# Output projection by tiles with the transposes among its products, and a last norm whose transposes and scaling are spread over three engines

## The reference

```
x = x + mix @ w_out
h = rmsnorm(x, norm_ffn_g)
q = h @ peer_w_q                     # 16 query parts of 128 columns
s = q . sub_keys, top 16 of 128 each # then pairs, gates by softmax
x = x + sum over 16384 experts: gate * gelu(u . h) * v
y = rmsnorm(x, norm_final_g)
```

## Time and profile before

| | before |
|---|---|
| three runs, us | 2292.63, 2301.97, 2316.4 |
| median, us | 2301.97 |
| span of the profiled execution, us | 2299.7 |
| mean granted TensorE clock | 0.955 |
| TensorE busy, us | 2145.2 |
| VectorE busy, us | 1526.3 |
| ScalarE busy, us | 713.2 |

### The profile page before, as it was taken

The page is one execution under the profiler, slowest core; times in us unless marked ns, Lnnn a source line. Parts: engine busy times, 40 slices in busy tenths (PEclk is TensorE's granted clock), DMA queues, the critical chain, the costliest instruction groups (busy, mean ns, idle before and its releaser), DMA issues.

```text
span 2299.7 us, 34370 instructions
## 1 busy us (share of the span) xinstructions
PE 2145.2 (93%) x13939; PEld 1759.0 (76%) x13939; DVE 1526.3 (66%) x2722; ACT 713.2 (31%) x859; POOL 393.5 (17%) x348
## 2 busy tenths in 40 slices
PE   5999998777789998999999999999999999999995
PEld 2545555656654676988989889989899999999995
DVE  2113355676642589888899899898676666666664
ACT  2112232334211201333444444445322222222221
POOL 4000000000000000022233223122332333333330
PEclk8999987778899999999999999999999999999998
DMA  5120110000212211457778779778998888888862
GB/s 183 37 74 19 48 57 14 2 7 2 80 48 106 75 41 38 149 200 268 290 285 316 279 273 335 277 259 293 370 353 309 310 310 310 310 308 311 314 251 97
DMA packets 164278, 437.38 MB, mean 190 GB/s; under 512 B 11968, under 2 KB 77248, under 8 KB 153792
## 3 DMA queue, kind: packets, MB, share of 16 engines
q1 hardware_dynamic: 116064, 242.81, 30.2%
q0 software_dynamic: 36864, 134.23, 15.7%
q10 hardware_dynamic: 11232, 58.73, 6.2%
HBM read 368.57 MB, written 67.17 MB: 189 GB/s over the span
## 4 chain that ended last, share of the span: by engine, by line
PE 56%; DVE 12%; ACT 2%; issue 1%; DMA 0%; POOL 0%; ACTq 0%; DVEq 0%
PE bank L1600 27%; PE bank L1538 21%; PE bank L1547 3%; PE bank L1465 3%; DVE sc L2097 1%; DVE si L2096 1%; DVE si L2099 1%; DVE u_lo L2104 1%; DVE isel L2239 1%; DVE sv L2095 1%; DVE sv L2098 1%; DVE sca L2110 1%; DMA sca<-in_pu_rows,pick 0%; ACT u_hi L921 0%; PE bank L1519 0%
## 5 line engine op out<-in xcount | busy, mean ns | idle before, releaser
L1538 PE MATMUL bank<-xhi,u_hi 128*128 128x448 f32 x1024 | 385.7, 377 | 8.3 <-DVE u_lo L2104 7.7
L1600 PE MATMUL bank<-w_hi,v_hi 128*128 128x448 f32 x1024 | 375.0, 366 | 5.5 <-DVE w_lo L2342 5.5
L1538 PE MATMUL bank<-xhi,u_lo 128*128 128x448 f32 x1024 | 375.5, 367 | 0.0
L1538 PE MATMUL bank<-xlo,u_hi 128*128 128x448 f32 x1024 | 375.0, 366 | 0.0
L1600 PE MATMUL bank<-w_lo,v_hi 128*128 128x448 f32 x1024 | 374.7, 366 | 0.0
L1600 PE MATMUL bank<-w_hi,v_lo 128*128 128x448 f32 x1024 | 374.6, 366 | 0.0
L619 POOL DMA_INDIRECT sca<-in_pu_rows,pick x128 | 173.2, 1353 | 728.8 <-DVE sdot L2110 441.5
L619 POOL DMA_INDIRECT rows_v<-in_pv,pick x128 | 196.1, 1532 | 430.5 <-DVE xs L2324 384.3
L2348 DVE TENSOR_TENSOR v_lo<-v_raw,v_hi 128x4096 fp32r<-128x4096 f32 x32 | 141.6, 4425 | 173.3 <-ACT v_hi L982 173.3
L982 ACT ACTIVATE v_hi<-v_raw 128x4096 fp32r<-128x4096 f32 x32 | 116.1, 3627 | 428.6 <-PE bank L1600 409.6
L1051 PE MATMUL bank<-xnT,wbuf 128*128 128x512 f32 x416 | 230.8, 637 | 0.0
(11 more groups left out here) (524 smaller groups left out, 3103.4 us busy)
## 6 DMA issues: line engine op xcount, KB each, us to landing
u_raw<-in_pu SPq DMA_DIRECT2D x64, 1024.0 KB, 5.0
v_raw<-in_pv SPq DMA_DIRECT2D x32, 2048.0 KB, 17.0
act_scratch<-actb ACTq DMA_DIRECT2D x64, 448.0 KB, 6.0
gate_scratch<-gst ACTq DMA_DIRECT2D x14, 2048.0 KB, 8.7
wts<-act_scratch SPq DMA_DIRECT2D x32, 896.0 KB, 4.8
gring<-gate_scratch SPq DMA_DIRECT2D x32, 896.0 KB, 8.5
wbuf<-in_w_in SPq DMA_DIRECT2D x4, 2048.0 KB, 10.2
wring<-in_w_q SPq DMA_DIRECT2D x4, 2048.0 KB, 8.5
```

The source lines that it names most:

```text
L1538: ins = mm(bank[b][:, 0:DS], lhsT, rhs[:, 0:DS], **on)
L1600: ins = mm(bank[c][:, 0:DS], lhsT, rhs[q][:, e, :], **on)
```

## The change

In the passage the output projection runs tile by tile: `jj` 0 and 1 are tile 0, and so on. The transposes of a tile (`turn_back`) stand among the products: tile 0's behind `jj` 7, tile 1's behind 8, tile 2's behind 9. VectorE normalises tiles 0 and 1 ahead of adding tile 3, and 2 and 3 ahead of adding tile 4. The first two query parts begin with their first 288 columns (`q_half`), with the transposes of tiles 3 and 4 between. ScalarE copies `xhi` behind the third query part.

At the end the gathered tile is finished first, in the time of the last sums. The blocks of the first four banks, first halves of the rows, are turned back behind the fifth sum, those of the fifth and sixth bank behind the seventh, the rest at the end. Rows are added and squared by halves; ScalarE adds up the first half's square (through the bias of the root), VectorE multiplies the first half by the gain ahead of time into `y_half`, and ScalarE applies the row factor to it (`half_out`), while VectorE scales the second half.

```diff
         sq_late = v_raw1[:, D:2 * D]
+        y_half = [v_raw1[:, 2 * D + 512 * t:2 * D + 512 * t + 512] for t in range(4)]
+        SCALED = [1, 4, 6, 8, 9]
+        ROOT = [1, 2, 3, 5, 7]
...
             sp.wait_ge(s_x1s, 16 * 5)
-            for t, (t0, n) in enumerate(FTILES):
+            for t in ORDER:
                 sp.dma_start(x1_late[t][0:n, :], x1_d[t0:t0 + n, :]).then_inc(s_x1, 16)
-            for t, (t0, n) in enumerate(FTILES):
-                sp.wait_ge(S("y_ready"), t + 1)
+            for pos, t in enumerate(ORDER):
+                sp.wait_ge(S("y_ready"), pos + 1)
+                sp.wait_ge(S("yrms_ready"), SCALED[pos])
...
                 pass
-            for t, (t0, n) in enumerate(FTILES):
-                act.wait_ge(S("x1_ready"), 6 + t)
+            def row_rms(t):
+                act.wait_ge(S("x1_ready"), 2 * t + 2)
...
                 own(S("frms_ready"))
-            for t, (t0, n) in enumerate(FTILES):
+            def columns_out(t):
...
                     ins = act.activation(xfT[:, 4 * half:4 * half + 4, t0:t0 + n],
-                                         bank[4 + 2 * (t % 2) + half][:, 0:4 * n].rearrange("p (k n) -> p k n", k=4), ACT.Copy)
+                                         bank[6 - 2 * (t % 2) + half][:, 0:4 * n].rearrange("p (k n) -> p k n", k=4), ACT.Copy)
...
                 own(S("xfT_ready"))
-            act.activation(xhi[:, :, :], xfT[:, :, 0:DS], ACT.Copy).then_inc(S("xhi_ready"), 1)
+            for t in range(4):
+                row_rms(t)
+            columns_out(0)
+            columns_out(1)
+            row_rms(4)
+            for t in range(2, 5):
+                columns_out(t)
...
                 act.activation(qT[:, j, HN:NT], bank[b + 1][:, 0:HN], ACT.Copy).then_inc(S("qT_ready"), 1)
+                if j == 2:
+                    act.activation(xhi[:, :, :], xfT[:, :, 0:DS], ACT.Copy).then_inc(S("xhi_ready"), 1)
...
                     high_weights(i, g)
-            for t, (t0, n) in enumerate(FTILES):
-                act.wait_ge(S("x2_ready"), t + 1)
-                link(act.activation(sq_late[0:n, :], x1_late[t][0:n, :], ACT.Square, accum_out=st[0:n, t, 2:3]))
-                act.activation(st[0:n, t, 3:4], st[0:n, t, 2:3], ACT.Sqrt, bias=eps_t[0:n, 0:1], scale=1.0 / D
+            n = FTILES[4][1]
+            act.wait_ge(S("x2_ready"), 1)
+            link(act.activation(sq_late[0:n, :], x1_late[4][0:n, :], ACT.Square, accum_out=st[0:n, 4, 2:3]))
+            act.activation(st[0:n, 4, 3:4], st[0:n, 4, 2:3], ACT.Sqrt, bias=eps_t[0:n, 0:1], scale=1.0 / D
+                           ).then_inc(S("yrms_ready"), 1)
+            own(S("yrms_ready"))
+            halves = [slice(0, 512), slice(512, D)]
+            for t, (t0, n) in enumerate(FTILES[0:4]):
+                act.wait_ge(S("x2_ready"), t + 2)
+                link(act.activation(sq_late[0:n, halves[0]], x1_late[t][0:n, halves[0]], ACT.Square, accum_out=st[0:n, t, 2:3]))
+                link(act.activation(st[0:n, t, 2:3], st[0:n, t, 2:3], ACT.Identity, bias=eps_t[0:n, 0:1], scale=1.0 / D))
+            def half_out(t):
+                act.wait_ge(S("y_ready"), t + 2)
+                act.activation(x1_late[t][0:n, halves[0]], y_half[t][0:n, :], ACT.Copy, scale=st[0:n, t, 3:4]
...
                 own(S("yrms_ready"))
+            for t, (t0, n) in enumerate(FTILES[0:4]):
+                act.wait_ge(S("x2_ready"), t + 6)
+                link(act.activation(sq_late[0:n, halves[1]], x1_late[t][0:n, halves[1]], ACT.Square, accum_out=st[0:n, t, 0:1]))
+                act.activation(st[0:n, t, 3:4], st[0:n, t, 0:1], ACT.Sqrt, bias=st[0:n, t, 2:3], scale=1.0 / D
+                               ).then_inc(S("yrms_ready"), 1)
+                own(S("yrms_ready"))
+                if t:
+                    half_out(t - 1)
+            half_out(3)
...
             def out_product(jj, kt):
-                half, t = divmod(jj, 5)
+                t, half = divmod(jj, 2)
...
             pe.wait_ge(S("mix_ready"), 8)
+            def turn_back(t):
+                pe.wait_ge(S("xf_ready"), t + 1)
+                if t == 1:
+                    pe.wait_ge(S("x1_ready"), 6)
+                if t >= 2:
+                    pe.wait_ge(S("xfT_ready"), t - 1)
+                for kt in range(KD):
+                    ins = pe.transpose(bank[6 - 2 * (t % 2) + kt // 4][:, n * (kt % 4):n * (kt % 4) + n],
+                                       xf_rows(t)[0:n, 128 * kt:128 * kt + 128], ident[0:n, 0:n])
+                ins.then_inc(S("xfT_done"), 1)
...
                 ins.then_inc(S("outproj_done"), 1)
-            for t, (t0, n) in enumerate(FTILES):
-                pe.wait_ge(S("xf_ready"), t + 1)
-                if t >= 2:
-                    pe.wait_ge(S("xfT_ready"), t - 1)
+                if jj >= 7:
+                    turn_back(jj - 7)
+            def q_half(j, half):
+                pp, b = j // 4, 2 * (j % 2)
                 for kt in range(KD):
-                    ins = pe.transpose(bank[4 + 2 * (t % 2) + kt // 4][:, n * (kt % 4):n * (kt % 4) + n],
-                                       xf_rows(t)[0:n, 128 * kt:128 * kt + 128], ident[0:n, 0:n])
-                ins.then_inc(S("xfT_done"), 1)
+                    ins = mm(bank[b + half][:, 0:HN], wring[:, pp % 2, kt, 128 * (j % 4):128 * (j % 4) + 128],
+                             xfT[:, kt, HN * half:HN * half + HN], start=kt == 0, stop=kt == KD - 1)
+                return ins
+            pe.wait_ge(s_ring[0], 16 * 2)
+            pe.wait_ge(S("x1_ready"), 10)
+            pe.wait_ge(S("xfT_ready"), 3)
+            for j in range(2):
+                q_half(j, 0)
+                turn_back(3 + j)
             pe.wait_ge(S("xfT_ready"), 5)
-            pe.wait_ge(S("x1_ready"), 10)
+            for j in range(2):
+                q_half(j, 1).then_inc(S("qproj_done"), 1)
...
                 ins.then_inc(S("scores_done"), 1)
-            for j in range(16):
+            scores(0)
+            for j in range(2, 16):
...
                 pe.wait_ge(s_ring[pp % 2], 16 * (pp // 2 + 2))
-                if j >= 2:
-                    pe.wait_ge(S("qT_ready"), j - 1)
+                pe.wait_ge(S("qT_ready"), j - 1)
...
                 ins.then_inc(S("qproj_done"), 1)
-                if j:
-                    scores(j - 1)
+                scores(j - 1)
...
             pe.wait_ge(S("gmat_copied"), DS // 4 + 2)
+            def turn_half(t, kts, half):
+                for kt in kts:
+                    ins = pe.transpose(bank[t][0:n, 128 * (kt % 4):128 * (kt % 4) + 128],
+                                       acc[:, kt, FTILES[t][0]:FTILES[t][0] + n], ident[:, :])
+                return ins
...
                     ins.then_inc(S("sum_done"), 1)
+                    if last and c == 4:
+                        pe.wait_ge(S("sum_banks_free"), 4)
+                        for t in range(4):
+                            turn_half(t, range(0, 4), 0).then_inc(S("back_done"), 1)
+                    if last and c == 6:
+                        pe.wait_ge(S("sum_banks_free"), 6)
+                        pe.wait_ge(S("x2_ready"), 5)
+                        for t in range(4):
+                            turn_half(t, range(4, 6), 1)
...
             sums(0, EG - 1, last=True)
+            pe.wait_ge(S("sum_banks_free"), 7)
+            for t in range(4):
+                turn_half(t, (6,), 1)
             pe.wait_ge(S("sum_banks_free"), KD)
-            for t, (t0, n) in enumerate(FTILES[0:4]):
-                for kt in range(KD):
-                    ins = pe.transpose(bank[2 * t + kt // 4][0:n, 128 * (kt % 4):128 * (kt % 4) + 128],
-                                       acc[:, kt, t0:t0 + n], ident[:, :])
-                ins.then_inc(S("back_done"), 1)
+            for t in range(4):
+                turn_half(t, (7,), 1).then_inc(S("back_done"), 1)
...
             dve.wait_ge(s_x1, 16 * 5)
-            for half in range(2):
-                for t, (t0, n) in enumerate(FTILES):
-                    jj = 5 * half + t
+            def add_rows(t):
+                for half in range(2):
+                    jj = 2 * t + half
...
                     own(S("x1_ready"))
-            dve.wait_ge(s_sub, 32)
-            for t, (t0, n) in enumerate(FTILES):
+            def norm_rows(t):
...
                 own(S("xf_ready"))
+            add_rows(0)
+            add_rows(1)
+            add_rows(2)
+            dve.wait_ge(s_sub, 32)
+            norm_rows(0)
+            norm_rows(1)
+            add_rows(3)
+            norm_rows(2)
+            norm_rows(3)
+            add_rows(4)
+            norm_rows(4)
...
                     sample_add(4 * g + r)
-            for c in range(KD):
+            def bank_out(c):
...
                 dve.tensor_copy(acc[:, c, 0:DS], bank[c][:, 0:DS]).then_inc(S("sum_banks_free"), 1)
+            def scale_rows(t, cs, root):
+                dve.wait_ge(S("yrms_ready"), root)
```

(51 more changed lines are left out.)

7 lines of the change are left out of this document (added).

## The result

| | before | changed |
|---|---|---|
| median, us | 2309.89 (20 runs, 2292.57 to 2319.74) | 2291.57 (20 runs, 2277.42 to 2300.76) |
| span of the profiled execution, us | 2299.7 | 2285.1 |
| mean granted TensorE clock | 0.955 | 0.956 |

The ratio, taken over all runs, is 0.9931, 95% interval 0.9907 to 0.9954: 0.7% faster, inside the 1% bound. (The two medians alone give 0.9921.)

The account below looks back on a forecast made before the run. TensorE matmuls hold 56% of the chain, and the long loops, almost without idle time, stay untouched. Gains of 13.6 us (end) and 1.8 (passage), 15.4 together, off 2301.97 give 2286.5 us; range 2278 to 2300.

Parts of the forecast that it names:

- Search and chain: From VectorE's top-16 search on: the chain is VectorE until the first expert product, so the passage's gain arrives undiminished.
- (e): Rival, passage: TensorE's score cadence absorbs its gain, leaving 13.6 us and 2288.3 us; chance 0.05.
- Passage: Output projection to query projection: first query product 4.7 us earlier, part given back, gain 1.8 us taken.
- Clock: Passage, TensorE's clock: gain 3.5 us with no fall, 1.8 with a fall of the same length; fall taken.
- (a): Rival, passage: the clock doesn't fall, 1.7 us more gain, 2284.8 us; chance 0.20.
- Sub-keys: Passage, VectorE's first normalisation: sub-keys land at 736.2, cover just enough, cost 0 to 0.3 us.
- Cover at the end: Last sums: the fourth bank copy ends near 2262.2, TensorE wants it at 2263.8, slack 1.6 us.
- (b): Rival, last sums: the end's cover fails; gathered rows 5 us later cost 3.4 us, about 2290; chance 0.09.
- Turns: Last norm: ScalarE sets the pace, a turn of 1.8 us against 4.47 before.
- (c): Rival, end and passage: slower ScalarE-VectorE handovers, 2.4 us, and a passage stall of 1 us: 2290; chance 0.09.
- Store: Behind the last scaling: the store of 64 rows, kept at 3.0 us.

Follow-up runs that it names:

- e2: Kernel before with only the changed kernel's end, the passage left as before: 2291.08 us (11 runs), ratio 0.9932, passage 62.05 us.
- e3: Changed kernel, but ScalarE copies the third tile's columns ahead of the fifth tile's square and root: 2285.89 us, passage 58.34 us.
- e6: Changed kernel with three unused products of 512 columns on TensorE in the wait ahead of the first query product: 2275.92 us, passage 59.84 us.
- e4: Changed kernel with the sub-keys loaded ahead of the two weight panels: 2284.04 us, passage 59.08 us.
- e1: Kernel before with only the changed kernel's passage, the end left as before: 2304.35 us (12 runs), ratio 0.9984, passage 62.55 us.
- e5: Changed kernel with the sub-keys' load held back until eight output products are done: 2299.14 us, passage 69.32 us.

## Why the prediction was right

Forecast 2286.5 us against a before of 2301.97, a ratio of 0.9933; measured 0.9931, and 2291.57 us, within 2278 to 2300, with a before that came out 8 us higher too. That the ratios agree to 0.0002 is luck: the interval of 0.9907 to 0.9954 holds gains from 10.6 to 21.5 us. The stretches are what bears the forecast out. Step by step:

- **Search and chain**: search takes 137.24 and 137.28 us, so what the passage wins does arrive. (e) is refuted.
- **Passage**: first query product forecast at +39.6 behind the mixer, measured +39.04, since the last product ended 0.4 us sooner than summed (+35.4 for +35.8); the fifth tile's wait 1.2, measured 1.24; gain 1.8, measured 2.10 (61.24 for 63.34). This holds because both profiles have a fall of like price, 1.6 and 1.7 us; against e2's execution of the old passage the gain would be 0.8. The named order of ScalarE, root before columns, was the limit: e3 moved it and nothing else.
- **Clock**: I took the fall, and it came; e6 prices it at 1.7 us, the term I had (3.5 against 1.8). But behind the wait it was a draw: e4 escaped it, e1 had it twice as long, and before itself has a spread of 1.3 us (e2). Whether (a) comes is then a matter of the execution; the forecast's side of it came in seven of eight.
- **Sub-keys**: 0 to 0.3 us forecast, 0.41 measured: "just enough" was slightly too kind. The load landed as forecast, 18.09 us behind the mixer for 18.1 (the chain names 16.63 us of `subT<-in_sub`, up to 733.25), but VectorE's two steps took 0.2 us longer with their handovers, and TensorE was ready at +19.2 (e4) and not at +19.5. In the eight executions with the new passage and this load neither moved nor held back, the stall was 0.34 to 0.68 us. e4 and e5 confirm the cause from both sides.
- **Cover at the end**: slack forecast 1.6 us, seen 1.2, and TensorE didn't wait. (b) did not happen. Last banks forecast +2.8, measured +2.71: 24 transposes at their price.
- **Turns**: ScalarE's 1.8 us, measured 1.84. From the start of the last bank's copy to the end of the last scaling I summed 9.2 us (2273.8 to 2283.0); it was 9.52. The excess is three handovers of some 0.1 us each: from TensorE to VectorE's first addition, from ScalarE's last root to VectorE, and back for the last scaling. Of ScalarE's wait of 0.37 at that place my sum had 0.2. Handovers as in (c) thus cost 0.4 us, not 2.4.
- **Store**: 3.0 kept, 3.41 measured, which with the handovers is why the end fell short: 13.6 forecast, 12.99 measured.

13.6 + 1.8 = 15.4 forecast; 12.99 + 2.10 = 15.1 in the two stretches. That the spans differ by a similar 14.6 is luck, since -2.94 and +3.39 of foreign stretches cancel.

## What to carry to other kernels

A tail of strict turns between engines is shortened first by what can be done before the last input is there (transposes of finished banks, the tile whose input comes by another way), and only then by sharing the rest: 5.8 (with a fall of the clock in it) and 4.95 us against 0.9, each from one execution. When work is moved ahead, read the new order of the helper engine too: one ScalarE step in the wrong place cost 2.9 us with the fall of the clock behind it, more than the 2.1 that the passage had won. Judge a gain of some 0.2% by its stretch, cut at the same instructions in each trace, and by a second execution, not by the whole time.
